# Head norm moved to VectorE, an earlier second read of the decay bank, and maxima kept negated, in a two-block transformer kernel

## The reference

```python
# attention over selected keys: 8 heads of 64, 128 keys chosen per query
logits = einsum(q, k_sel) * 64 ** -0.5
p = softmax(where(valid, logits, -inf)); ya = einsum(p, v_sel) @ p_attn
# decays of the recurrence: 4 heads, keys of 128, values of 256
gate_logits = g_lr @ gla_w_gate + gla_b_gate
log_a = log_sigmoid(gate_logits) / 16
o = gla_chunked(gq, gk, gv, log_a)              # chunks of 64 tokens
# head norm and gate
mu = mean(o, axis=-1); var = mean((o - mu) ** 2, axis=-1)   # over the 256 of a head
o = (o - mu) * rsqrt(var + 1e-5) * gla_norm_g
yb = (o * silu(g_r)) @ p_gla
y = (sigmoid(gate_a) * ya + sigmoid(gate_b) * yb) @ w_out + b_out
```

## Time and profile before

| | before |
|---|---|
| median of 3 runs | 2964.12 us |
| runs | 2963.4 to 2969.92 us |
| profiled execution | 2959.03 us, span 2957.7 us |
| granted TensorE clock, mean | 0.979 |
| busy: TensorE, VectorE, ScalarE, GpSimd | 2789.0, 1241.4, 1106.9, 1069.7 us |
| moved by DMA | 269 MB, 91 GB/s |

### The profile page before, as it was taken

The page is one execution under the profiler, slowest core; times in us unless marked ns, Lnnn a source line. Parts: engine busy times, 40 slices in busy tenths (PEclk is TensorE's granted clock), DMA queues, the critical chain, the costliest instruction groups (busy, mean ns, idle before and its releaser), DMA issues.

```text
span 2957.7 us, 39008 instructions
## 1 busy us (share of the span) xinstructions
PE 2789.0 (94%) x15161; PEld 2291.5 (77%) x15161; DVE 1241.4 (42%) x2777; ACT 1106.9 (37%) x2069; POOL 1069.7 (36%) x854
## 2 busy tenths in 40 slices
PE   6999999989989899999899999999999989999997
PEld 5887878788768777766688888887776668888887
DVE  3344444444454437423325424255642332642425
ACT  3444444443444433443322433233335232242422
POOL 3333333223322233332344354435342235434442
PEclk9999999999999899999999999999999999999999
DMA  4322223241211222222244232323222224322222
GB/s 142 90 83 86 87 72 100 73 138 44 72 58 44 79 92 85 72 79 82 92 154 137 72 114 72 100 86 120 72 72 79 89 82 157 125 84 100 93 93 72
DMA packets 247547, 269.06 MB, mean 91 GB/s; under 512 B 11582, under 2 KB 208930, under 8 KB 246596
## 3 DMA queue, kind: packets, MB, share of 16 engines
q1 hardware_dynamic: 247364, 266.56, 27.7%
HBM read 247.59 MB, written 18.94 MB: 90 GB/s over the span
## 4 chain that ended last, share of the span: by engine, by line
PE 80%; DVE 8%; ACT 4%; POOL 3%; issue 3%; DMA 2%; SPq 0%; ACTq 0%; DVEq 0%; POOLq 0%
PE banks L1458 43%; PE banks L1455 24%; POOL WS L2685 3%; DVE AR L2118 2%; PE banks L1577 2%; PE banks L1476 2%; PE banks L1526 1%; PE banks L1684 1%; ACT WS L1784 1%; PE banks L1560 1%; DVE SM L2118 1%; PE banks L1500 1%; PE banks L1732 1%; PE banks L1662 1%; PE banks L1545 1%
## 5 line engine op out<-in xcount | busy, mean ns | idle before, releaser
L2685 POOL TENSOR_TENSOR WS<-WR,WS 128x512 fp32r<-128x512 f32 (+1 forms) x772 | 975.1, 1295 | 1579.6 <-ACT WS L1784 1579.6
L1458 PE MATMUL banks<-WS,UT 128*128 128x512 f32 (+1 forms) x5712 | 1218.1, 363 | 22.5 <-issue 5.5
L1458 PEld LDWEIGHTS banks<-WS,UT 128*128 128x128 f32 x5712 | 921.6, 192 | 199.8 <-issue 61.1
L1455 PE MATMUL banks<-UT,WS 128*128 128x512 f32 (+1 forms) x2928 | 690.9, 394 | 0.6 <-issue 0.6
L1455 PEld LDWEIGHTS banks<-UT,WS 128*128 128x128 f32 (+1 forms) x2928 | 547.8, 189 | 128.1 <-issue 13.5
L1784 ACT ACTIVATE WS<-WR 128x1024 fp32r<-128x1024 f32 (+2 forms) x408 | 395.1, 1021 | 121.0 <-PE banks L1458 63.2
L1458 PE MATMUL banks<-WS,AT 128*128 128x256 f32 (+1 forms) x1776 | 307.2, 334 | 20.3 <-DVE AT L2118 20.3
L1458 PEld LDWEIGHTS banks<-WS,AT 128*128 128x128 f32 x1776 | 267.9, 193 | 56.5 <-DVE AT L2118 15.8
L2648 DVE SCALAR_TENSOR_TENSOR AR<-banks,AR 128x511 f32<-128x511 f32 x88 | 66.0, 750 | 226.5 <-ACT AR L2098 226.5
L2118 DVE TENSOR_TENSOR AR<-AR 128x256 f32<-128x256 f32 (+2 forms) x165 | 144.9, 898 | 21.3 <-DMA AR<-spill 12.6
L2700 POOL TENSOR_TENSOR SM<-SM 128x1 f32<-128x1 f32 (+2 forms) x44 | 45.9, 1044 | 275.9 <-DVE SM L2624 120.5
(11 more groups left out here) (207 smaller groups left out, 2657.6 us busy)
## 6 DMA issues: line engine op xcount, KB each, us to landing
WR<-in_w_in SPq DMA_DIRECT2D x56, 1024.0 KB, 5.1
WR<-in_w_up SPq DMA_DIRECT2D x44, 1024.0 KB, 5.1
WR<-in_dil_w_in SPq DMA_DIRECT2D x128, 256.0 KB, 3.9
WR<-in_w_down SPq DMA_DIRECT2D x16, 1024.0 KB, 4.9
WR<-in_dil_w_in SPq DMA_DIRECT2D x8, 1024.0 KB, 5.2
WR<-in_diff_w_in SPq DMA_DIRECT2D x16, 512.0 KB, 4.3
WR<-in_diff_w_in SPq DMA_DIRECT2D x8, 1024.0 KB, 5.5
spill<-AR SPq DMA_DIRECT2D x32, 256.0 KB, 2.4
```

The costliest lines, as they stand in the source:

```text
L1455: mm = pe.matmul(B[bank][0:c, :], w[x][:, kk, g * P:g * P + c], act[:, y, kk, :], start=start, stop=stop)
L1458: mm = pe.matmul(B[bank][:, off:off + n], act[:, x, before_k + kk, g * P:g * P + P], w[y][:, kk, :], start=start, stop=stop)
L2685: ge.tensor_tensor(slot(i, 1)[:, s], raw(i)[:, s], slot(i, 0)[:, s].bitcast(F32), ALU.subtract).then_inc(lo_p.sem, 1)
```

## The change

It does four things. The selected scores are reduced as -0.125 x (score + mask) with a minimum, so that the exponential can take them with a scale of -1 and the minimum as bias; the negation goes, and the exponential of a head waits for that head's reduction alone. A decay's bank is read by VectorE as soon as ScalarE has taken its absolute value, into `la`, and the bank is free then; the logarithm is subtracted in `la` by a second instruction. The head norm is done on VectorE at the head of the gate step, four instructions of 128x256 with mean and rstd as scalars; ScalarE does none of it, the shift goes, and the statistics have two buffers. The gate's loads for blocks 0 and 1 are issued ahead of the statistics, those for blocks 2 and 3 right after the gate steps of blocks 0 and 1.

```diff
@@ -704,7 +704,6 @@
             def moments(b):
                 self.step("moments", l, b)
                 yield
-                self.step("centre", l, b)
 
             def gate(b):
                 self.step("gate_o", l, b)
@@ -714,6 +713,8 @@
                 self.step("turn", f"o{l}", b)
                 yield
 
+            for b in range(2):
+                self.step("load_gr", l, b)
             yield from self.staged(NB, [moments, gate, lambda b: (), turn])
             while "gb" not in on:
                 yield
...
@@ -1174,7 +1175,6 @@
                 for e in range(2):
                     freed[4 + e] = maxed.plan(("3", l, n + e))
                     exped.plan(("3", l, n + e))
-                negated.plan(("3", l, n))
             elif kind == "ranks":
                 k = takes_corner(("ranks", *a))
                 ones_set.plan(a[0])
@@ -1185,7 +1185,8 @@
                 takes(("decay", *a), bank)
                 decay_mm.plan(tuple(a))
                 soft.plan(tuple(a), 3)
-                freed[bank] = decayed.plan(tuple(a))
+                freed[bank] = lowered.plan(tuple(a))
+                decayed.plan(tuple(a))
             elif kind == "totals":
                 k = takes_corner(("totals", *a))
                 total_mm.plan(a[0])
@@ -1209,10 +1210,8 @@
             elif kind == "moments":
                 var_out.plan(("o", *a))
                 rstd.plan(("o", *a))
-            elif kind == "centre":
-                shift.plan(tuple(a))
-                centred.plan(tuple(a), 4)
             elif kind == "gate_o":
+                centred.plan(tuple(a))
                 gated_o.plan(tuple(a))
             elif kind == "gq":
                 freed[order.bank[a[0], a[1]][0]] = gq_out.plan((a[0], a[1]))
@@ -1985,12 +1984,12 @@
                 elif kind == "scores3":
                     l, n = a
                     w = P * (sel_units[n][0] + 1)
-                    se.wait_ge(negated.sem, negated.at["3", l, n])
                     for e in range(2):
                         v = arr(o_p + 512 * e, 512)[:, 0:w]
+                        se.wait_ge(maxed.sem, maxed.at["3", l, n + e])
                         if n >= 2:
                             se.wait_ge(recip.sem, recip.at["3", l, n + e - 2])
-                        se.activation(v, v, ACT.Exp, bias=SM[:, NBI + e:NBI + e + 1], scale=0.125,
+                        se.activation(v, v, ACT.Exp, bias=SM[:, MX + e:MX + e + 1], scale=-1.0,
                                       accum_out=SM[:, ZS + e:ZS + e + 1]).then_inc(exped.sem, 1)
 
                 elif kind == "turn3":
@@ -2042,13 +2041,6 @@
                     b, h = rec_units[n]
                     se.wait_ge(read_mm.sem, read_mm.at[l, n])
                     se.activation(XO[:, b, h, :], B[bank6["read", l, n]][:, 0:256], ACT.Copy).then_inc(read_out.sem, 1)
-
-                elif kind == "centre":
-                    l, b = a
-                    se.wait_ge(shift.sem, shift.at[l, b])
-                    for h in range(4):
-                        se.activation(XO[:, b, h, :], XO[:, b, h, :], ACT.Identity, bias=SM[:, SQ + 4 + h:SQ + 5 + h],
-                                      scale=SM[:, SQ + h:SQ + h + 1]).then_inc(centred.sem, 1)
 
                 elif kind == "gq":
                     i, half, l, j = a
@@ -2471,11 +2463,8 @@
                         if n >= 2:
                             ve.wait_ge(pturned.sem, pturned.at["3", l, n + e - 2])
                         ve.tensor_tensor_reduce(arr(o_p + 512 * e, 512)[:, 0:w], B[4 + e][:, 0:w],
-                                                SEL[b] if b else CT[:, C_KM:C_KM + P], 1.0, GONE, ALU.add, ALU.max,
-                                                SM[:, MX + e:MX + e + 1]).then_inc(maxed.sem, 1)
-                    ve.wait_ge(maxed.sem, maxed.at["3", l, n + 1])
-                    ve.tensor_scalar(SM[:, NBI:NBI + 2], SM[:, MX:MX + 2], -0.125, None,
-                                     ALU.mult).then_inc(negated.sem, 1)
+                                                SEL[b] if b else CT[:, C_KM:C_KM + P], -0.125, -GONE, ALU.add,
+                                                ALU.min, SM[:, MX + e:MX + e + 1]).then_inc(maxed.sem, 1)
 
                 elif kind == "turn3":
                     l, n = a
@@ -2496,9 +2485,11 @@
 
                 elif kind == "decay":
                     l, b = a
+                    ve.wait_ge(soft.sem, soft.at[l, b] - 2)
+                    ve.tensor_scalar(la[:, b, :], B[4 + b % 2][:, :], 0.0, None, ALU.min).then_inc(lowered.sem, 1)
+                    ve.wait_ge(lowered.sem, lowered.at[l, b])
                     ve.wait_ge(soft.sem, soft.at[l, b])
-                    ve.scalar_tensor_tensor(la[:, b, :], B[4 + b % 2][:, :], 0.0, tmps[b % 2], ALU.min,
-                                            ALU.subtract).then_inc(decayed.sem, 1)
+                    tt(la[:, b, :], la[:, b, :], tmps[b % 2], ALU.subtract).then_inc(decayed.sem, 1)
 
                 elif kind == "decayed_keys":
                     l, b = a
@@ -2529,10 +2520,10 @@
 
                 elif kind == "moments":
                     l, b = a
-                    st, mv = SM[:, ST:ST + 24], SM[:, MV:MV + 8]
+                    st, mv = SM[:, ST + 24 * (b % 2):ST + 24 * (b % 2) + 24], SM[:, MV + 8 * (b % 2):MV + 8 * (b % 2) + 8]
                     ve.wait_ge(read_out.sem, read_out.at[l, 4 * b + 3])
-                    if b > 0:
-                        ve.wait_ge(centred.sem, centred.at[l, b - 1])
+                    if b > 1:
+                        ve.wait_ge(centred.sem, centred.at[l, b - 2])
                     for h in range(4):
                         x = ve.bn_stats(st[:, 6 * h:6 * h + 6], XO[:, b, h, :])
                     x.then_inc(dve_step, 1)
@@ -2541,19 +2532,19 @@
                         x = ve.bn_aggr(mv[:, 2 * h:2 * h + 2], st[:, 6 * h:6 * h + 6])
                     x.then_inc(dve_step, 1)
                     ve.wait_ge(dve_step, V.of())
-                    ve.tensor_scalar(SM[:, SQ:SQ + 4], mv.rearrange("p (h s) -> p h s", s=2)[:, :, 1], LN_EPS, None,
+                    ve.tensor_scalar(SM[:, SQ + 4 * (b % 2):SQ + 4 * (b % 2) + 4],
+                                     mv.rearrange("p (h s) -> p h s", s=2)[:, :, 1], LN_EPS, None,
                                      ALU.add).then_inc(var_out.sem, 1)
-
-                elif kind == "centre":
-                    l, b = a
-                    ve.wait_ge(rstd.sem, rstd.at["o", l, b])
-                    ve.scalar_tensor_tensor(SM[:, SQ + 4:SQ + 8],
-                                            SM[:, MV:MV + 8].rearrange("p (h s) -> p h s", s=2)[:, :, 0], -1.0,
-                                            SM[:, SQ:SQ + 4], ALU.mult, ALU.mult).then_inc(shift.sem, 1)
 
                 elif kind == "gate_o":
                     l, b = a
                     xb = XO[:, b].rearrange("p h d -> p (h d)")
+                    mv, r = MV + 8 * (b % 2), SQ + 4 * (b % 2)
+                    ve.wait_ge(rstd.sem, rstd.at["o", l, b])
+                    for h in range(4):
+                        x = ve.tensor_scalar(XO[:, b, h, :], XO[:, b, h, :], SM[:, mv + 2 * h:mv + 2 * h + 1],
+                                             SM[:, r + h:r + h + 1], ALU.subtract, ALU.mult)
+                    x.then_inc(centred.sem, 1)
                     ve.wait_ge(centred.sem, centred.at[l, b])
                     ve.wait_ge(gr_in[b % 2], 32 * l + 16 * (b // 2 + 1))
                     tt(xb, xb, arr(13824 + 1024 * (b % 2), D), ALU.mult).then_inc(gated_o.sem, 1)
@@ -2693,7 +2684,7 @@
                     elif kind == "square2":
                         key, o, n = ("2", a[0]), SQ, 8
                     elif kind == "moments":
-                        key, o, n = ("o", *a), SQ, 4
+                        key, o, n = ("o", *a), SQ + 4 * (a[1] % 2), 4
                     else:
                         key, o, n = ("ln", *a[:3]), MV + 2 * a[2] + 1, 1
                     ge.wait_ge(var_out.sem, var_out.at[key])
@@ -2803,14 +2794,15 @@
                     sy.wait_ge(spill_act.sem, spill_act.at[i, half])
                     sy.dma_start(spill[l, :, o:o + 512], arr(o_y2 + 512 * half, 512)).then_inc(spilled[half].sem, 16)
 
-                elif kind == "moments":
+                elif kind == "load_gr" or kind == "gate_o" and a[1] < 2:
                     l, b = a
-                    if b == 0:
+                    if kind == "gate_o":
+                        sy.wait_ge(gated_o.sem, gated_o.at[l, b])
+                        b += 2
+                    elif b == 0:
                         for half in range(2):
                             sy.wait_ge(spilled[half].sem, spilled[half].at[index[f"m{l}gr1"], 2 + half])
                         sy.wait_ge(summed.sem, summed.at["3", l, N3 - 1])
-                    if b >= 2:
-                        sy.wait_ge(gated_o.sem, gated_o.at[l, b - 2])
```

(4 more changed lines are left out.)

## The result

| | before | after |
|---|---|---|
| median | 2966.39 us of 4 runs | 2944.52 us of 4 runs |
| runs | 2963.4 to 2969.92 | 2939.99 to 2947.25 |
| profiled execution | 2959.03, span 2957.7 | 2947.25, span 2945.9 |
| granted TensorE clock | 0.979 | 0.982 |

The ratio is 0.9932, 95% interval 0.9918 to 0.9946: faster by 16 to 24 us. I predicted 2947.4 from a median of 2964.1, 16.7 us less; measured are 21.9 us between medians.

A forecast was written before the change was run, and what follows sets the result against it. TensorE, busy 94% of the span, was taken to bound the kernel, so only its idle time counted. Gains of 1.2 + 5.1 + 10.4 = 16.7 us took the median from 2964.1 to 2947.4 us; own range 2941 to 2952, with rivals 2935 to 2957.

The forecast's parts named there:

- part B with A: Early read of decay banks, with the selected maxima's share at unit 24: 5.1 us gained over both layers, bounds 3 to 9.
- part C: Head norm moved to VectorE in the gate step: 5.2 us gained in each layer, 10.4 us in all.
- A, first units: Selected maxima, first unit of each layer: 0.6 of TensorE's 1.65 us wait on the exponential goes, 1.2 us for two layers.
- B with A at unit 24: TensorE's wait for the exponential at unit 24 ends earlier: 2.2 us gained in layer 0, 2.9 in layer 1.
- C, wait ahead of block 1: Head norm: TensorE idles 1.8 us before block 1's transposes in place of 6.67.
- C, wait ahead of block 2: Head norm: TensorE idles 3.6 us before block 2's transposes.
- C, norm 2 beside GpSimd: Block 2's four VectorE norm passes each wait out one GpSimd weight subtraction: four times 1.26 us plus 0.3.
- Rival 1: Head norm: no collision of the two-scalar passes with GpSimd; gain 9.8 us a layer, 25.9 in all, 2938.2 us; chance 25%.
- The chain I named: Unit 24's exponential waits on a spill behind a weight load, GpSimd's subtraction and unit 22's exponentials; these start 1.4 us earlier.
- 2: Rival: following weight subtractions also meet block 3's norm, 5 us more before its transposes; gain 8.3 us, 2955.8 us; chance 15%.
- 3: Rival: TensorE's gaps reopen at the next supply, such as weight tiles; less than 5.9 us left, about 2961 us; chance 7%.
- 4: Rival: GpSimd holds all four head norms of a layer; 13.3 us slower, 2977.4 us; chance 3%.

The follow-up runs named there:

- second profile: The kernel after, unchanged, run and profiled once more: 2943.65 us (5 runs), ratio 0.9932 against the kernel before.
- ga1 held: Kernel after, with GpSimd's low-half subtractions for one weight tile waiting until block 2's head norm is done: 2953.7 us, ratio 0.996 against before.
- maxima alone: Kernel before with only the negated maxima and the exponential's wait per head: 2956.69 us (5 runs), ratio 0.9971.
- decays alone: Kernel before with only the early read of the decay's bank: 2962.45 us (10 runs), ratio 0.9989.
- spills first: Kernel after with one weight tile's load kept back until the gate's first two spills are issued: 2938.96 us (4 runs), ratio 0.9906 against before.

## Why the prediction was right

**The time.** 2944.5 against 2947.4, in my case's own range. That it came so near is in part luck: part B with A gave about half of its term, part C more than its own, and the two errors of some 2.5 us each cancel. The steps, as the two profiles and the stretches show them:

| step | predicted | shown |
|---|---|---|
| A, first units | 1.2 us | 1.1 us (0.93 and 1.25 left of two times 1.65) |
| B with A at unit 24, layers 0 / 1 | 2.2 / 2.9 us | 2.6 / 3.2 us up to unit 24; 2.6 / -1.0 us to the end of the stretch; second profile 1.0 / 1.7 |
| C, wait ahead of block 1 | 1.8 us | 1.78, 1.75 us |
| C, wait ahead of block 2 | 3.6 us | 2.94, 2.92 us |
| C, norm 2 beside GpSimd | 6.2 us | 5.27 us |
| C, gain a layer | 5.2 us | 4.9 and 6.4; second profile 7.5 and 6.4 us |

**Part C** was right in mechanism and nearly so in size. Norm 2 met ga1's subtractions, each pass took the length of one of them (5.27 for four), and undisturbed it took 1.38 for four, the 1.4 I had from both near rows. Rival 1, no collision, is refuted by this and by the runs with ga1 held. I charged a quarter of a microsecond too much a pass, since I added VectorE's own time to GpSimd's 1.26, where the four passes and the four subtractions together took 5.27. The Trainium skill's rule (SBUF — State Buffer, section on who interferes with whom) is a lock of the shared pair for the whole instruction. The trace agrees with it in the pace, one pass for each subtraction. It does not agree in the sum: if each engine waited out the whole of the other's instructions, four subtractions and four passes would take 5.0 + 1.4 = 6.4 us by my estimate, and GpSimd took 5.18 here against 5.01 for its next four. Why the passes cost it almost nothing stays open. The gain was 1.2 us larger a layer than my 5.2 in mean (6.4), from the shorter second wait and less halved clock.

**Part B with A** was right up to unit 24 and wrong behind it. The chain I named is the one in the trace. In the kernel before, the spill's issue stood right behind the load's, 15.67 us behind decay 0's products:

```profile
1296.45 1.12 PE L1702 MATMUL banks<-MF,AR 17*128 17x512 f32 x2
...
1311.70 0.37 SPq L2716 DMA_DIRECT2D WR<-in_w_in  x1
...
1312.12 1.07 SPq L2798 DMA_DIRECT2D spill<-AR  x2
```

In after it came at 13.93, so 1.7 us earlier where I had 1.4, and TensorE was 2.6 and 3.2 us early at unit 24 where I had 2.2 and 2.9. The step that failed is "Layer 0: 2.2 us, layer 1: 2.9 us" as what stays: I gave the new, longer wait at unit 24 no price in clock. In layer 1 of the profiled execution these rows stand behind it:

```profile
2256.24 0.66 PE L1672 MATMUL banks<-CT,AR 128*128 128x128 f32 x4 [2.42 <-ACT AR L1992]
...
2259.21 2.07 PE L1701 MATMUL banks<-MF,AR 17*128 17x512 f32 x2
```

```profile
2257.50:2265.00 7.50, 7.50 (x20) 4.78 (x19) 2.62 (x6) 5.38 (x7) 5.23 (x4) 0.50 0.13 39
```

From 2257.5 to 2265 TensorE is busy without a gap at half its clock, which costs 3.75 us (5.1 with its edges) and takes back more than the 3.2. So the sum of B with A in the stretches was 1.6 us in one pair of profiles and 2.8 in the other, 2.5 by the means, not 5.1. It is the rule and not the exception: behind that wait the clock falls in eleven of twelve layers. The single-part runs fit: maxima alone and decays alone bring the stretch to 49.3 to 49.9, and both together to no less in mean (50.5). What sets it is the spill, and the run with the spills first shows it by going to 45.1 at full clock.

**The sum** of the steps in the first pair of profiles is 1.1 + 1.6 + 11.3 = 14.0 us, of which 11.8 us are in the spans; the untouched stages differ by 2 to 3 us either way. The second profile of after (span 2938.1) stands 19.6 below that of before. By the means it is 1.1 + 2.5 + 12.8 = 16.4 us, so that some 5 of the 21.9 us between medians have no place in these stretches; whether they are halved clock elsewhere or the spread between runs stays open.

**The rivals.** 2 was closest to deciding: norm 3 missed the next subtractions, and where one hold made it meet them the kernel lost 8 to 10 us by the medians. 3 came true in part, at unit 24. 4 did not: of eight norms two met GpSimd.

## What to carry to other kernels

Look at what stands ahead of a copy in the queue of its engine before asking how fast the copy is: moving the norm behind the copy was worth nearly all of part C, on either engine. After each wait taken away, follow TensorE to its next supplier and ask what the longer wait there costs in clock as well as in idle time: here one wait of 2.4 us was taken away, and at the next supplier a wait of 2.2 to 2.4 us with a halved clock behind it stood in its place. A small store on which an engine waits should be issued ahead of a large load that nobody needs yet: here the swap took 5.4 us from each decay stretch in mean, where the earlier read of the decays alone had taken 1.0 and 1.8.

## What the runs showed of the hardware beyond that

- VectorE passes of one fp32 SBUF input and two scalars from SBUF took 1.38 us for four of 128x256 where nothing met them. Beside GpSimd's subtractions of 128x512 four took 5.27 and 4.36 us, the 128x1024 product 2.17 instead of 1.23, and the addition on 128x4 0.66 instead of 0.17. The head statistics took 1.40 beside them, as alone. Which instructions of VectorE stand still differs by instruction.
- Who starts first seems to pass first. With ga1 held, gate 2 started at 1448.79 and took 1.22 us as alone; GpSimd's four subtractions, issued 0.05 later, took 6.07 instead of 5.0 to 5.2. Where the subtractions were first by 0.06 us (1446.48, norm 2 at 1446.54), VectorE paid and GpSimd took 5.18.
- How much halved clock follows a wait differs from one execution of the same program to the next: behind the same wait of 2.9 us in layer 0's norm, block 2's transposes took 1.94 us in one profile and 1.16 in the other. Behind unit 24's wait of 2.2 to 2.4 us it followed in eleven of twelve layers, for 3 to 10 us. A single trace can't tell what a wait of that length costs in clock; a dozen such places can.
